# A compression's position term: from 32 one-column TensorE products to a GpSimd multiply-and-add tree with two column sums

## The reference

```python
def compress(k, pos_emb, w1, w2):
    n_cmp = (k.shape[2] - CMP_BLOCK) // CMP_STRIDE + 1
    idx = jnp.arange(n_cmp)[:, None] * CMP_STRIDE + jnp.arange(CMP_BLOCK)[None, :]
    blocks = k[:, :, idx] + pos_emb
    flat = blocks.reshape(*blocks.shape[:3], CMP_BLOCK * HEAD_DIM)
    return jax.nn.gelu(flat @ w1) @ w2
...
kc = compress(k_cmp, cmp_pos_k, cmp_w1_k, cmp_w2_k)
vc = compress(v_cmp, cmp_pos_v, cmp_w1_v, cmp_w2_v)
```

## Time and profile before

| | |
|---|---|
| median of 3 runs | 1730.13 us (1729.81 to 1732.28) |
| the profiled execution's own time | 1729.57 us |
| its span | 1727.8 us |
| TensorE busy | 1605.6 us (93%) |
| VectorE busy | 1037.5 us (60%) |
| GpSimd busy | 520.9 us (30%) |
| L963 and L969 together | from 866.73 to 889.78 us of the span |

### The profile page before, as it was taken

One profiled execution on the slowest core, in us unless ns is written; L12 is line 12 of the kernel. 1 busy time (PEld: TensorE's weight loads), 2 busy tenths in 40 slices (PEclk: granted clock), 3 DMA queues, 4 the chain that ended last, 5 costly groups with the idle time before them and its releaser, 6 DMA issues.

```text
span 1727.8 us, 21319 instructions
## 1 busy us (share of the span) xinstructions
PE 1605.6 (93%) x7204; PEld 1265.9 (73%) x7204; DVE 1037.5 (60%) x1557; ACT 441.9 (26%) x960; POOL 520.9 (30%) x387
## 2 busy tenths in 40 slices
PE   4797788869899999999899999999999899999998
PEld 4676677648677778878797666666888788888886
DVE  8756898665777777554635555476645544444433
ACT  5312333551211111110313444444111322222101
POOL 1787342003699999554500000000002000000011
PEclk8888988769999999999979999999999999999999
DMA  8455222003356556444412111110333233333332
GB/s 285 146 156 148 83 77 62 12 1 109 111 176 185 172 170 183 138 113 136 124 28 73 37 37 37 37 50 25 98 98 97 73 97 97 97 95 92 94 92 91
DMA packets 325505, 174.24 MB, mean 101 GB/s; under 512 B 7818, under 2 KB 321348, under 8 KB 325444
## 3 DMA queue, kind: packets, MB, share of 16 engines
q1 hardware_dynamic: 325444, 173.44, 34.5%
HBM read 171.32 MB, written 2.10 MB: 100 GB/s over the span
## 4 chain that ended last, share of the span: by engine, by line
PE 49%; ACT 2%; DVE 1%; issue 0%; ACTq 0%; DVEq 0%
PE bank L617 10%; PE bank L619 10%; PE bank L618 10%; PE bank L1042 6%; PE bank L876 3%; PE bank L1109 3%; PE bank L885 1%; PE bank L969 1%; PE bank L963 1%; PE bank L631 1%; ACT wt L1336 1%; PE bank L632 0%; PE bank L633 0%; PE bank L1100 0%; PE bank L1009 0%
## 5 line engine op out<-in xcount | busy, mean ns | idle before, releaser
L617 PE MATMUL bank<-uh,wh 128*128 128x512 f32 x920 | 365.3, 397 | 5.1 <-DVE wl L1532 3.8
L1530 DVE CAST wh<-wraw 128x1024 fp32r<-128x1024 f32 (+1 forms) x235 | 225.3, 959 | 229.6 <-PE bank L619 211.2
L619 PE MATMUL bank<-uh,wl 128*128 128x512 f32 x920 | 361.2, 393 | 0.0
L618 PE MATMUL bank<-ul,wh 128*128 128x512 f32 x920 | 361.2, 393 | 0.0
L1532 DVE TENSOR_TENSOR wl<-wraw,wh 128x1024 fp32r<-128x1024 f32 (+1 forms) x235 | 327.9, 1395 | 8.1
L505 POOL TENSOR_TENSOR ssq<-sq 128x512 f32<-128x512 f32 x4 | 8.7, 2175 | 854.6 <-ACT sq L1158 854.6
L535 POOL TENSOR_TENSOR ada<-ada 128x512 f32<-128x512 f32 (+1 forms) x160 | 219.7, 1373 | 12.6
L617 PEld LDWEIGHTS bank<-uh,wh 128*128 128x128 f32 x920 | 174.8, 190 | 43.9 <-issue 3.8
L530 POOL TENSOR_TENSOR ada<-ada,sc_c 128x1024 f32<-128x1024 f32 x80 | 159.4, 1992 | 155.6 <-DMA ada<-in_w_ada_dram 155.4
L619 PEld LDWEIGHTS bank<-uh,wl 128*128 128x128 f32 x920 | 174.5, 190 | 37.1
L618 PEld LDWEIGHTS bank<-ul,wh 128*128 128x128 f32 x920 | 174.6, 190 | 35.3
(11 more groups left out here) (322 smaller groups left out, 2525.8 us busy)
## 6 DMA issues: line engine op xcount, KB each, us to landing
ada<-in_w_ada_dram SPq DMA_DIRECT2D x92, 512.0 KB, 5.0
wraw<-in_w_in_dram SPq DMA_DIRECT2D x66, 512.0 KB, 3.7
wraw<-in_w_ffn_gate_dram SPq DMA_DIRECT2D x44, 512.0 KB, 3.8
wraw<-in_w_ffn_up_dram SPq DMA_DIRECT2D x44, 512.0 KB, 3.7
wraw<-in_w_ffn_down_dram SPq DMA_DIRECT2D x32, 512.0 KB, 3.8
wraw<-in_w_out_dram SPq DMA_DIRECT2D x16, 512.0 KB, 3.6
wraw<-in_w_ffn_down_dram SPq DMA_DIRECT2D x16, 384.0 KB, 3.3
xin<-in_x_dram SPq DMA_DIRECT2D x4, 512.0 KB, 5.6
```

Source lines behind the costliest of these rows:

```text
L617: nc.tensor.matmul(bank[:], a, rh[:, k0 + k, :], start=(first and k == 0), stop=False)
L618: nc.tensor.matmul(bank[:], a, rl[:, k0 + k, :], start=False, stop=False)
L619: mm = nc.tensor.matmul(bank[:], b, rh[:, k0 + k, :], start=False, stop=(last and k == nk - 1))
L1530: V.tensor_copy(wh[:, slot, 0:n], wraw[:, slot, 0:n]).then_inc(w_hi, 1)
```

## The change

GpSimd multiplies all 16 tiles of `w1c[:, n]`, 2048 elements a partition, by the embeddings, each spread over its tile's 128 columns, and adds the 16 tiles together in a tree (1024, 512, 256, 128 elements). What is left, `wfin[:, n]`, is a 128 by 128 tile whose sum over the partitions is the position vector. TensorE makes that sum by one product with a column of ones, in place of the sixteen. The ten GpSimd instructions stand before the tables; they wait for `c_in` (the weights' loads) and, since `wpos` lies over the tiles of the raw square sums, for `r_sum`. A new semaphore `c_pos` counts them: five steps a half.

```diff
--- before.py
+++ after.py
@@ -184,6 +184,8 @@
         w2c = at("w2c", [P, 3, HD], where=s_at + 2 * K2)
         hc = at("hc", [P, 2, GROUPS, CPAD], where=s_at + 3 * K2)
         hcr = at("hcr", [P, GROUPS, REP, CPAD], where=s_at + 3 * K2 + 512)
+        wpos = at("wpos", [P, 16, P], where=s_at + 5 * K2)
+        wfin = at("wfin", [P, 2, P], where=s_at + 2 * K2 + 1024)
         hx = at("hx", [P, 2, GROUPS * NCMP], where=s_at + 4 * K2)
         z2 = at("z2", [P, 2, ZW], where=s_at)
         wt2 = at("wt2", [P, NT, T], where=s_at + 5 * K2)
@@ -270,7 +272,7 @@
         pair_ok, mh_ok, ml_ok = sem("pair_ok"), sem("mh_ok"), sem("ml_ok")
 
         c_in, tab2, c_h, c_hb, c_hx, c_hg = (sem("c_in"), sem("tab2"), sem("c_h"), sem("c_hb"), sem("c_hx"), sem("c_hg"))
-        c_kv, c_kvc = sem("c_kv"), sem("c_kvc")
+        c_kv, c_kvc, c_pos = sem("c_kv"), sem("c_kvc"), sem("c_pos")
         c_z, c_v, c_e, c_t, c_wt = sem("c_z"), sem("c_v"), sem("c_e"), sem("c_t"), sem("c_wt")
         v2_turn, v2_turned = sem("v2_turn"), sem("v2_turned")
         y_f, y_h, y_l = sem("y_f"), sem("y_h"), sem("y_l")
@@ -573,6 +575,17 @@
             add_raw_square(KT - 1)
 
             g.wait_ge(n_ul, KT * 3)
+            g.wait_ge(r_sum, 1)
+            g.wait_ge(c_in, 64)
+            for n, pos in enumerate((POS_K, POS_V)):
+                if n:
+                    g.wait_ge(c_pos, 5)
+                nc.gpsimd.tensor_tensor(wpos[:], w1c[:, n], vt2[:, pos:pos + 16].unsqueeze(2).broadcast_to([P, 16, P]),
+                                        ALU.mult).then_inc(c_pos, 1)
+                for level, k in enumerate((8, 4, 2, 1)):
+                    g.wait_ge(c_pos, 5 * n + level + 1)
+                    dst = wpos[:, 0:k] if k > 1 else wfin[:, n:n + 1]
+                    nc.gpsimd.tensor_tensor(dst, wpos[:, 0:k], wpos[:, k:2 * k], ALU.add).then_inc(c_pos, 1)
             m = [0]
 
             def step2(ins):
@@ -964,11 +977,9 @@
                                      w1c[:, n, jj, :],
                                      kds[:, n, :, 2 * jj:2 * jj + CSTRIDE * (NCMP - 1) + 1:CSTRIDE],
                                      start=(jj == 0), stop=False, skip_group_check=True)
-                pos = (POS_K, POS_V)[n]
-                for jj in range(16):
-                    mm = nc.tensor.matmul(B[4 + n][:, CPAD * GROUPS:CPAD * GROUPS + 1], w1c[:, n, jj, :],
-                                          vt2[:, pos + jj:pos + jj + 1], start=False, stop=(jj == 15),
-                                          skip_group_check=True)
+                pe.wait_ge(c_pos, 5 * n + 5)
+                mm = nc.tensor.matmul(B[4 + n][:, CPAD * GROUPS:CPAD * GROUPS + 1], wfin[:, n, :], ones[:, 0:1],
+                                      start=False, stop=True, skip_group_check=True)
                 mm.then_inc(c_h, 1)
             simple("qa2", uh, ul, part=(1, 2))
```

## The result

The changed kernel took 1710.43 us (median of 4 runs, 1704.85 to 1716.03); the kernel before 1729.97 us (4 runs, 1725.33 to 1732.28). The ratio is 0.9906, 95% interval 0.9878 to 0.9935: some 16 us faster, 11 to 21. (The two medians alone would give 0.9887, which lies in the interval.) Forecast were 1719.0 us and a range down to 1714.0, so the gain is larger than forecast. The change was run again with the experiments: 0.9889 (0.9863 to 0.9916).

A forecast was written before the change was run, and what follows sets the result against it. TensorE, never idle between 866.73 and 895 us, was taken as the bound. 12.75 + 0.6 - 2.2 = 11.15 us off gave 1719.0 us against the median, with an 8-in-10 range of 1714.0 to 1723.0.

The forecast's parts named there:

- Removed: TensorE's compression: 64 position-product records go, two products come; 128 records become 68, 23.05 us become 10.3, gain 12.75 us.
- The clock stays up: Rival, TensorE's compression: full clock throughout, 68 records take 7.5 us, 16.0 us gained in all, 1714.1 us; chance 0.08.
- 68 records, 10.3 us: TensorE's compression: 41 records at 0.111 us, then the clock falls and 27 run at 0.215, 10.3 us in all.
- Dense unit, gain 0.6: TensorE's dense unit behind the compression: loss to the low clock falls from 2.65 to 2.05 us, gain 0.6 (0 to 1.1).
- GpSimd, 17.2 us: GpSimd's added multiply and additions: 8.6 us for each of keys and values, 17.2 us for both.
- The split, 2.2 us late: VectorE's split for qa2's second unit waits out GpSimd's instructions, so TensorE starts that unit 2.2 us late.
- the rival of a late GpSimd: Before the values' sum: TensorE waits 6.0 us, 1725.0; or milder lateness or a clock fall near 861, about 1721.6; chance 0.15.
- Waits for c_pos, nothing: TensorE's waits before the key and value sum products cost nothing, the second by 2.6 us.
- Tables, nothing: GpSimd's tables move to about 876.2 to 886.9 us; first wanted about 907.7, 21 us of cover, so no cost.
- The gain arrives whole: Behind the compression: what TensorE gains there arrives at the end nearly whole; its longest total wait after 890 us is 2.5.

The follow-up runs named there:

- the wide version: On the kernel before: the 32 one-column position products made 62 columns wide, nothing new on GpSimd; 1714.46 us, ratio 0.9925.
- the deferred version: On the changed kernel: VectorE's splits for qa2's second and fourth units earlier, GpSimd waiting for the former, sum products after qa2's third unit; 1710.15 us, ratio 0.9898.
- the kernel with both: On the kernel before: GpSimd's ten instructions added, their result unused, TensorE still making the 32 one-column products; 1725.98 us, ratio 0.9992.

## Why the prediction was wrong

The step that failed is the clock in "Removed": "I take the same 4.5 us: 41 records at 0.111, then 27 at 0.215". I took the fall as a matter of how long narrow products had run. The runs show that it was a matter of which: 62-column products held the clock for 7 to 14 us in each of the eight profiles that have so long a run of them, and it fell 1.0 to 3.5 us into runs of one-column products in the kernel before and in three experiments. The rival "The clock stays up", with a chance of 0.08, was the case: it gave 16.0 us, the distances show 16.56; its stretch of 7.5 us was 7.51; 1714.1 us stood against 1713.7 by the measured ratio (0.9906 of 1729.97). Its parts were off by little: 2.52 for its 2.65 behind the compression, 1.5 for its 2.2 at the split.

The evidence that I held against this rival did not bear on it. That 62-column products at 0.50 do not bring the clock back says nothing of whether they hold it at 1.00. And the run of 32-column products did not lose the clock within itself in the kernel before, as I had read it. It was over when the next weight unit began, and the clock fell at 919.02, 0.37 us into that unit:

```profile
918.65 0.50 PE L617 MATMUL bank<-uh,wh 128*128 128x512 f32 x1
```

```profile
919.02:922.40 3.38, 3.38 (x10) 2.64 (x9) 3.31 (x4) 0.00 (x0) 0.00 (x0) 0.50 0.00 0
```

Nor does it fall there every time. In eight of the ten profiles it fell in that run or just behind it; in the wide and in the deferred version it stayed at 1.00. These are the same run and the unit behind it in the wide version:

```profile
901.93:905.62 3.69, 3.69 (x65) 3.65 (x64) 0.00 (x0) 1.88 (x2) 0.00 (x0) 1.00 0.01 2
905.62:910.00 4.38, 4.38 (x21) 3.65 (x20) 4.12 (x5) 0.36 (x1) 0.00 (x0) 1.00 0.00 0
```

So what is shown is the difference between 1 and 62 columns. Where between them the clock is lost was not tested; the 32-column run, whose operands also have 64 rows instead of 128, went either way.

Point by point:

- *68 records, 10.3 us:* 68 records, 7.51 us. The price of a record, 0.111 us at the full clock, was right. Wrong by 2.8 us: the clock.
- *Dense unit, gain 0.6:* 2.52 from the unit's start to the scores (25.17 before, 22.65 now), since it now runs at 1.00; half of 5.29 gave 2.65. Wrong by 1.9 us, the same cause.
- *GpSimd, 17.2 us:* the multiply took 3.61 where undisturbed (3.8 forecast); both halves with their waits lasted 20.3 us, where the forecast had 21.3 (854.9 to 876.2). That they were done at 876.17 and the forecast said 876.2 is chance: every start of this execution is 1.5 us late.
- *The split, 2.2 us late:* the distance grew by 1.5 us, of which 1.19 idle. Mechanism right, size not: the multiply ended 3.5 us after the subtraction before it, not 3.8, so it was over almost when the cast was due, and the cast lost next to nothing instead of 0.7. The clock did not fall in the new idle time, which the rival of a late GpSimd had feared: in all five profiles with that wait it stayed at 1.00.
- *Waits for c_pos, nothing:* right, with 0.9 us to spare at the second. Forecast were 2.6, with a clock that falls; at the full clock the rival had it just in time.
- *Tables, nothing:* right; they ended 17.6 us before L2013 wanted them at 903.77.
- *The gain arrives whole:* right, 812.85 against 812.81 us.

The gain by cause, from the profiles: keeping the clock is worth 11.4 us (the wide version, with all 128 records), the 60 records fewer 14.21 - 7.51 = 6.7 us, and the collision takes back 1.5. That makes 16.6, as measured.

## What to carry to other kernels

A TensorE stretch of tiny products is priced by its clock as much as by its records: look up the granted clock over it and behind it, and ask which products hold it, before counting instructions. A fall seen in a mixed run has to be put down to one part of it by an experiment (here a broadcast operand, one line), not to its length. When GpSimd is given elementwise work, look for VectorE's next cast, copy or subtraction in SBUF, and count up to one whole GpSimd instruction as its delay. And look at more than one profile before a clock is called kept or lost.

## What was not expected of the hardware

62-column products kept the clock at 1.00 for 14.25 us, yet at 0.50 they did not bring it back in 6.87 us, in the kernel before and again in the kernel with both. The clock is also not the same in every execution: in the deferred version's it fell in qa2's first unit, behind eight one-column sums and a wait of 1.11 us, where the profile of the changed kernel, with the same sums and the same wait, kept 1.00.

And a small instruction waits like a large one, while others do not wait at all. These rows are the deferred version's, with GpSimd multiplying from 854.96 to 858.57:

```profile
854.96 3.61 POOL L584 TENSOR_TENSOR wpos<-w1c,vt 128x2048 f32<-128x2048 f32 x1 [21.42 <-DVE wl L1549]
```

```profile
856.05 0.18 DVE L1994 RECIPROCAL tiny<-tiny 128x4 f32<-128x4 f32 x1 [1.27 <-ACT tiny L1410]
856.21 0.17 DVE L1995 MEMSET hc<- 128x128 f32 x1
856.41 2.21 DVE L1998 COPY w2c<-w2c 128x64 f32<-128x64 f32 x1
```

VectorE's copy of 64 columns, 0.20 us in the kernel before, took 2.21 and ended just behind the multiply. The reciprocal and the memset took 0.18 and 0.17 us, as in the kernel before.
